# Second attention of a hybrid encoder step: values as the stationary operand for pairs of heads, normalised by a block diagonal product

## The reference, cut to what matters

```python
def stick_breaking(q, k, v, qpos, kpos):              # 8 heads of 64
    z = einsum('bqhd,bkhd->bhqk', q, k) * B_DIM ** -0.5
    before = kpos[None, :] < qpos[:, None]
    log_keep = where(before, log_sigmoid(-z), 0.0)
    rev = cumsum(log_keep, axis=3, reverse=True)
    after = concatenate([rev[..., 1:], zeros_like(rev[..., :1])], axis=-1)
    a = where(before, exp(log_sigmoid(z) + after), 0.0)
    return einsum('bhqk,bkhd->bqhd', a, v)

oa = rms(oa) * p['g_sub_a'] * (1.0 - lam_init)        # first attention, 4 heads of 128
ob = rms(ob) * p['g_sub_b']                           # rms over the 64 elements of one head
o = concatenate([oa.reshape(b, t, 512), ob.reshape(b, t, 512)], axis=-1) @ p['w_out']
x = x + g1 * o
```

## Time and profile before

| | |
|---|---|
| median of 3 runs | 1126.28 us (1124.11 to 1126.4) |
| profiled execution | 1125.94 us, span 1124.1 us |
| PE busy | 1060.9 us (94%) |
| PEld busy | 661.9 us (59%) |
| DVE busy | 395.1 us (35%) |
| ACT busy | 276.9 us (25%) |
| POOL busy | 293.7 us (26%) |
| mean granted clock of TensorE | 0.988 of full speed |
| second attention, from its first scores | 252.24 to 348.66 us of the span |

### The profile page before, as it was taken

The page is one execution under the profiler, slowest core; times in us unless marked ns, Lnnn a source line. Parts: engine busy times, 40 slices in busy tenths (PEclk is TensorE's granted clock), DMA queues, the critical chain, the costliest instruction groups (busy, mean ns, idle before and its releaser), DMA issues.

```text
span 1124.1 us, 19352 instructions
## 1 busy us (share of the span) xinstructions
PE 1060.9 (94%) x6520; PEld 661.9 (59%) x6521; DVE 395.1 (35%) x954; ACT 276.9 (25%) x735; POOL 293.7 (26%) x494
## 2 busy tenths in 40 slices
PE   3999999999998999999999999989999999999994
PEld 1677755556765447765656555656666565656541
DVE  3633301655754227422222222222222222222447
ACT  3200004667653005012111111111111111111232
POOL 1000002003521000523434334334433434333300
PEclk9999999999999999999999999999999999999997
DMA  8722245007740008479899999999999999998394
GB/s 333 286 75 75 76 169 183 1 1 286 281 150 1 1 0 314 193 313 392 321 336 416 415 415 415 414 415 401 380 356 359 407 413 414 415 400 349 121 418 119
DMA packets 77649, 304.26 MB, mean 271 GB/s; under 512 B 13302, under 2 KB 15416, under 8 KB 59496
## 3 DMA queue, kind: packets, MB, share of 16 engines
q1 hardware_dynamic: 60696, 268.26, 61.2%
q0 software_dynamic: 16256, 33.08, 7.8%
q10 hardware_dynamic: 656, 2.36, 0.5%
HBM read 290.26 MB, written 33.82 MB: 288 GB/s over the span
## 4 chain that ended last, share of the span: by engine, by line
PE 56%; DMA 4%; SPq 4%; issue 2%; DVE 1%; POOL 1%; ACT 1%; ACTq 0%; POOLq 0%; DVEq 0%
PE bank L1100 24%; PE bank L1107 13%; PE bank L1022 5%; DMA arena<-in_w_down 4%; PE bank L1093 3%; PE bank L1174 3%; PE bank L1112 2%; PE bank L1165 1%; SPq L384 1%; SPq L383 1%; PE bank L708 1%; PE bank L709 1%; POOL arena L561 1%; SPq L387 1%; PE bank L954 1%
## 5 line engine op out<-in xcount | busy, mean ns | idle before, releaser
L1100 PE MATMUL bank<-arena 128*64 128x256 f32 x2880 | 332.3, 382 | 16.4 <-issue 8.7
L1100 PEld LDWEIGHTS bank<-arena 128*64 128x64 f32 x2880 | 248.2, 138 | 123.6 <-issue 67.3
L1918 DVE COPY arena<-bank 128x512 f32<-128x512 f32 x90 | 62.2, 691 | 328.7 <-PE bank L1093 328.7
L1107 PE MATMUL bank<-arena 128*64 128x512 f32 x728 | 176.3, 601 | 1.5 <-DVE arena L1912 0.6
L1429 ACT COPY arena<-bank 128x128 f32<-128x128 f32 x90 | 23.9, 266 | 413.4 <-PE bank L1112 413.4
L576 POOL DMA_INDIRECT arena<-h_rows,arena x93 | 98.4, 1058 | 82.7 <-POOL arena L573 78.2
L584 POOL DMA_INDIRECT y_rows<-arena x91 | 93.4, 1026 | 85.7 <-POOL arena L581 79.3
L757 PE MATMUL bank<-arena 128*128 128x288 f32 x448 | 108.9, 406 | 0.3 <-DVE arena L1578 0.3
L757 PEld LDWEIGHTS bank<-arena 128*128 128x128 f32 x448 | 85.0, 190 | 24.5 <-issue 1.1
L1912 DVE COPY arena<-bank 128x512 f32<-128x512 f32 x91 | 62.9, 691 | 102.2 <-PE bank L1107 102.2
L1107 PEld LDWEIGHTS bank<-arena 128*64 128x64 f32 x728 | 52.1, 136 | 67.1 <-issue 66.4
(11 more groups left out here) (289 smaller groups left out, 1100.4 us busy)
## 6 DMA issues: line engine op xcount, KB each, us to landing
arena<-in_w_gate SPq DMA_DIRECT2D x64, 1024.0 KB, 12.7
arena<-in_w_up SPq DMA_DIRECT2D x64, 1024.0 KB, 15.4
arena<-in_w_down SPq DMA_DIRECT2D x64, 1024.0 KB, 14.5
arena<-in_w_ada SPq DMA_DIRECT2D x8, 2048.0 KB, 12.0
arena<-in_w_in SPq DMA_DIRECT2D x5, 2048.0 KB, 8.1
arena<-y_rows SPq DMA_DIRECT2D x3, 3072.0 KB, 16.7
arena<-in_w_ada SPq DMA_DIRECT2D x8, 1024.0 KB, 17.8
arena<-in_w_out SPq DMA_DIRECT2D x2, 2048.0 KB, 9.7
```

Of the source, the lines that this page charges most:

```text
L1100: last = pe.matmul(bank[0][n * SLOT:n * SLOT + SLOT, 0:2 * P].rearrange("p (g f) -> p g f", f=P), HGT[:, k % 4, k // 4, :], w[:, :, n * P: ...
L1107: last = pe.matmul(bank[3][n * SLOT:n * SLOT + SLOT, :], AE[:, f, :], DN[j][:, f, 512 * n:512 * n + 512], start=(f == 0), stop=(f == 1))
L1918: dve.tensor_copy(hgt, bank[1][:, :]).then_inc(hgt_ready, 1)
```

## The change

The weights A of a head are in SBUF with keys on the partitions. Before, A was the stationary operand and the head's values V (64 columns) the moving one, ten products for each head. Now `pair_values(p)` makes V stationary (128x64) and streams A (512, 384, 256 and 128 columns for the four key blocks), with the two heads of a pair in the two column halves of the array, so the outputs come out transposed in bank 7: head elements on the partitions, 512 queries on the free dimension.

ScalarE copies them straight to OT (`pair_out`, 128x512). VectorE squares them into SQ, TensorE multiplies SQ by PAIR, a block diagonal matrix of 1/64 (`pair_squares`), which puts each head's mean square on all its partitions, ScalarE takes Ln and then Exp with scale -0.5 (`pair_root`), and VectorE multiplies output, root and gain (`pair_norm`). The transposes of k = 4 to 7 of the prompt and their copies go, as do all `b_mean`, `b_rms`, `b_norm` of the prompt heads; the sample keeps the old way.

TensorE's order for a pair is now `b_scores`, `pair_values(p-1)`, `ada` twice, `b_sums` twice, `pair_squares(p-1)`. ScalarE does `pair_root(p-1)` after the pair's last Exp, VectorE `pair_norm(p-2)` and `pair_square(p-1)` after the pair's logarithms. Pair 3's values come after `b_scores(8)`, its squares after `b_sums(8)` and ahead of the gate rows, its root on ScalarE ahead of the sample's copies.

```diff
@@ TensorE
+            def pair_values(p):
+
+                if p:
+                    pe.wait_ge(pair_ln, PAIR_BASE + p)
                 else:
                     pe.wait_ge(proj_dve, NT)
-                if h in (HB - 2, HB - 1):
+                if p == HB // 2 - 1:
                     unread(7)
+                pe.wait_ge(at_ready, 6 * p + 6)
+                for j in range(4):
+                    for h in (2 * p, 2 * p + 1):
+                        o = h % 2 * DB
+                        last = pe.matmul(bank[7][o:o + DB, j * P:TP], V[:, j, 512 + h * DB:512 + h * DB + DB], AT[:, h % 2, ZO[j]:ZO[j] + ZW[j]],
+                                         start=(j == 0), stop=(j == 3), skip_group_check=True)
+                last.then_inc(pvb_done, 1)
+
+            def pair_squares(p):
+
+                pe.wait_ge(ob_evac, p + 1)
+                pe.wait_ge(pair_sq, PAIR_BASE + p + 1)
+                pe.matmul(bank[7][:, :], PAIR, SQ, start=True, stop=True).then_inc(pair_ms, 1)
...
                 if p:
-                    b_values(2 * p - 1)
+                    pair_values(p - 1)
...
-                if p < HB // 2 - 1:
-                    b_values(2 * p)
+                if p:
+                    pair_squares(p - 1)
             b_scores(HB)
-            b_values(HB - 2)
+            pair_values(HB // 2 - 1)
             ada_turn_later()
-            b_values(HB - 1)
             b_sums(HB)
+            pair_squares(HB // 2 - 1)
...
-            turn(OA, 1, half=(on_ready, NT + HB), sample=(on_ready, NT + HB + 1))
+            for k in range(4):
+                turn_chunk(OA, k, 2)
+            turn_sample(OA, (on_ready, NT + 1))
             turned(1)
+            pe.wait_ge(pair_ready, PAIR_BASE + HB // 2)
@@ ScalarE
+            def pair_out(p):
+                act.wait_ge(pvb_done, p + 1)
+                act.copy(OT[:, 4 + p, 0:TP], bank[7][:, :]).then_inc(ob_evac, 1)
+
+            def pair_root(p):
+
+                act.wait_ge(pair_ms, PAIR_BASE + p + 1)
+                act.activation(SQ, bank[7][:, :], ACT.Ln, bias=EPST[:, 0:1]).then_inc(pair_ln, 1)
+                act.wait_ge(pair_ln, PAIR_BASE + p + 1)
+                act.activation(SQ, SQ, ACT.Exp, scale=-0.5).then_inc(pair_rs, 1)
...
                 if p:
-                    b_out(2 * p - 1)
+                    pair_out(p - 1)
                 b_exp(2 * p)
                 b_exp(2 * p + 1)
-                if p < HB // 2 - 1:
-                    b_out(2 * p)
+                if p:
+                    pair_root(p - 1)
             b_fade(HB)
-            b_out(HB - 2)
+            pair_out(HB // 2 - 1)
             b_log(HB)
-            b_out(HB - 1)
             b_exp(HB)
-            b_out(HB)
+            pair_root(HB // 2 - 1)
+            b_out()
@@ VectorE
+            dve.memset(EPST, EPS)
+            for o in (0, DB):
+                dve.memset(PAIR[o:o + DB, o:o + DB], 1.0 / DB)
+                dve.memset(PAIR[o:o + DB, DB - o:P - o], 0.0)
...
+            def pair_square(p):
+
+                dve.wait_ge(ob_evac, p + 1)
+                o = OT[:, 4 + p, 0:TP]
+                dve.tensor_tensor(SQ, o, o, ALU.mult).then_inc(pair_sq, 1)
+
+            def pair_norm(p):
+
+                dve.wait_ge(pair_rs, PAIR_BASE + p + 1)
+                o = OT[:, 4 + p, 0:TP]
+                dve.scalar_tensor_tensor(out=o, in0=o, scalar=GA[:, 1:2], in1=SQ, op0=ALU.mult, op1=ALU.mult).then_inc(pair_ready, 1)
+                dve.wait_ge(pair_ready, PAIR_BASE + p + 1)
...
+                if p >= 2:
+                    pair_norm(p - 2)
                 if p:
-                    b_mean(2 * p - 2)
-                    b_mean(2 * p - 1)
-                if p >= 2:
-                    b_norm(2 * p - 4)
-                    b_norm(2 * p - 3)
+                    pair_square(p - 1)
...
             b_keep(HB)
-            b_mean(HB - 2)
-            b_mean(HB - 1)
-            b_norm(HB - 2)
-            b_norm(HB - 1)
+            pair_square(HB // 2 - 1)
+            pair_norm(HB // 2 - 1)
             b_mean(HB)
```

More of the change, by code:

```diff
@@ L158, in build @@
         GA = at(take(2), 2)
+        PAIR = at(take(P), P)
+        EPST = at(take(1), 1)
         SS = at(take(NT), NT)
@@ L265, in build @@
         z_half = sem("z_half")
+        pair_sq, pair_ms, pair_ln, pair_rs, pair_ready = ada_ld[0], ada_ld[1], ada_ld[6], ada_ld[7], in0_ld[0]
+        PAIR_BASE = 16
         abs_ready, fade_ready, ls_ready, z_done, lk_ready, p_done, eb_done, at_ready, pvb_done, ob_evac, lk_ln = map(
@@ L624, in back, with turn_chunk, turn @@
                 return last
-            def turn_chunk(src, k):
+            def turn_chunk(src, k, step=1):
                 for t in range(4):
                     last = pe.transpose(bank[k % 4][:, t * P:t * P + P], src[:, t, k * P:k * P + P], IDENT)
-                last.then_inc(tr_done, 1)
-            def turn(src, r, half=None, sample=None, begun=0, only_prompt=False):
+                last.then_inc(tr_done, step)
+            def turn(src, r, begun=0, only_prompt=False):
                 for k in range(begun, KC):
-                    if k == 4 and half:
-                        pe.wait_ge(*half)
                     if k >= 4:
@@ L642, in turn @@
                 if not only_prompt:
-                    turn_sample(src, sample)
+                    turn_sample(src)
             def turn_sample(src, sample=None, odd_apart=False):
@@ L955, in on_rows, with b_values @@
                 return last
-            def b_values(h):
-                if h >= 1:
-                    pe.wait_ge(ob_evac, h)
+            def pair_values(p):
+                if p:
+                    pe.wait_ge(pair_ln, PAIR_BASE + p)
                 else:
                     pe.wait_ge(proj_dve, NT)
-                if h in (HB - 2, HB - 1):
+                if p == HB // 2 - 1:
                     unread(7)
[L965 to L972, removed]
+                pe.wait_ge(at_ready, 6 * p + 6)
[9 more added lines that the diff above has]
+                pe.matmul(bank[7][:, :], PAIR, SQ, start=True, stop=True).then_inc(pair_ms, 1)
+            def b_values(h):
+                pe.wait_ge(pair_ln, PAIR_BASE + HB // 2)
+                pe.wait_ge(at_ready, 3 * HB + 1)
+                if h == HB:
                     pe.wait_ge(eb_done, 3 * HB + 3)
@@ L1205, in squares, with turned @@
                 act.activation(junk[0:r, :], X[0:r, t, :], ACT.Square, accum_out=SS[0:r, t:t + 1]).then_inc(done, 1)
-            def turned(r, dst, scale, shift, ks=range(1, KC, 2)):
+            def turned(r, dst, scale, shift, ks=range(1, KC, 2), step=1):
                 for k in ks:
-                    act.wait_ge(tr_done, 9 * r + k + 1)
+                    act.wait_ge(tr_done, 9 * r + step * (k + 1))
                     if scale:
@@ L1214, in turned @@
                         ins = act.copy(dst[:, k, 0:TP], bank[k % 4][:, :])
-                    ins.then_inc(tr_act, 1)
+                    ins.then_inc(tr_act, step)
             act.wait_ge(smt_ready, 1)
@@ L1340, in b_exp, with b_out @@
                     if h >= 2 and x == 0:
-                        act.wait_ge(pvb_done, h - 1)
+                        act.wait_ge(pvb_done, h // 2)
                     act.activation(AT[0:r, h % 2, o:o + w], b[0:r, 0:w], ACT.Exp).then_inc(eb_done, 1)
[L1344 to L1350, removed]
+            def pair_out(p):
[6 more added lines that the diff above has]
+                act.activation(SQ, SQ, ACT.Exp, scale=-0.5).then_inc(pair_rs, 1)
+            def b_out():
+                act.wait_ge(pvb_done, HB // 2 + 1)
+                act.copy(OA[0:TS, 4, 512:768], bank[7][0:TS, 0:256])
+                act.copy(OA[0:TS, 4, 768:D], bank[7][TS:P, 0:256]).then_inc(ob_evac, 1)
             for p in range(HB // 2):
@@ L1507, in norm, with turned @@
                 dve.tensor_scalar(XN[0:r, t, :], X[0:r, t, :], RS[0:r, t:t + 1], None, ALU.mult).then_inc(xn_ready, 1)
-            def turned(r, dst, scale, shift, ks=range(0, KC, 2)):
+            def turned(r, dst, scale, shift, ks=range(0, KC, 2), step=1):
                 for k in ks:
-                    dve.wait_ge(tr_done, 9 * r + k + 1)
+                    dve.wait_ge(tr_done, 9 * r + step * (k + 1))
                     if shift:
@@ L1515, in turned @@
                     elif scale:
-                        dve.tensor_scalar(dst[:, k, 0:TP], bank[k % 4][:, :], scale(k, 0), None, ALU.mult).then_inc(tr_dve, 1)
+                        dve.tensor_scalar(dst[:, k, 0:TP], bank[k % 4][:, :], scale(k, 0), None, ALU.mult).then_inc(tr_dve, step)
                     else:
                         dve.tensor_copy(dst[:, k, 0:TP], bank[k % 4][:, :]).then_inc(tr_dve, 1)
-                if r == 2 or KC - 2 not in ks:
+                if r == 2 or ks[-1] != (2 if r == 1 else KC - 2):
                     return
@@ L1738, in b_norm @@
             def b_norm(h):
-                dve.wait_ge(orb_ready, h + 1)
```

(1 more changed line is left out.)

18 lines of the change are left out of this document (6 added, 12 removed).

## The result

| | before | after |
|---|---|---|
| median | 1126.30 us (8 runs) | 1133.74 us (8 runs, 1131.67 to 1140.49) |
| ratio, 95% interval | | 1.0079 (1.0063 to 1.0095) |
| profiled execution / its span | 1125.94 / 1124.1 | 1132.37 / 1130.6 |
| PE busy | 1060.9 | 1057.9 |
| ACT busy | 276.9 | 289.4 |

The change makes the kernel slower by 7.4 us, going by the medians. (The ratio gives 8.9 us, since two of the eight times are 1137.50 and 1140.49.) In the windows by stage the reader is to see first that the pairs are as forecast, and then the clock. They answer to the earlier trace rows: pairs 1, 2 and 3, the sample's scores up to `b_sums(8)`, from there to the end of the sample's values, and the turn with the second gate rows. Columns are length, busy PE, PEld, DVE, ACT, POOL, granted clock, DMA share, GB/s.

A forecast was written before the change was run, and what follows sets the result against it. TensorE was taken as busy throughout the attention, with the logarithm chain ending within 0.1 us of it. Pairs -0.20, sample +1.03, turn -0.33 gave +0.5; one clock fall, 1.6, made +2.1: 1128.4 us, range 1124.5 to 1132.

The forecast's parts named there:

- tiles not side by side: Rival: the two halves of `pair_values` run one after the other, 4.4 us instead of 2.36; 1133.4 us, chance 0.04.
- TensorE's work, the pairs: Attention pairs: TensorE's own work falls some 8.8 us, but waits for VectorE and ScalarE leave the four pairs at -0.20.
- TensorE keeps its savings: Rival: the logarithms don't bind, so TensorE's 8.8 us are kept, 1117.5, or half, 1122; chance 0.12.
- Table loads: ScalarE's root in each pair: two table loads, one before Ln and one before Exp, 1.28 us each.
- Sample part and turn without the clock: Sample part +1.03 us, with 3.35 idle ahead of `b_sums(8)`; turn -0.33 us, from 16 fewer transposes.
- A fall costs 1.6: One added fall to 1.2 GHz behind the sample part's idle stretch: 16 products take 3.63 us instead of 2.05.
- Bounds 0 to 3.2: Clock term: 0 if the fall is missed, 3.2 if it also catches pair 1's stall or lasts longer in the turn.
- a bound and a rival: Longer or further falls, in pair 1 or the turn: bound 3.2 us; rival up to 1.6 more, 1130.0, chance 0.16.
- no further fall: Rival: the sample part's idle stretch is split so that the clock stays; +0.5, 1126.8 us, chance 0.20.
- one load: Rival: ln then exp need one table load, so each root is 1.28 us or more shorter; 1127.1, chance 0.03.
- savings case: Rival that TensorE's savings are kept in full (1117.5 us) or half (1122); chance 0.12, of which 0.09 counted as faster.
- half of the forecast: Whole kernel: half the forecast's 0.45 chance, counted as within 0.2% (2.25 us), since its centre is 2.1.

The follow-up runs named there:

- e7_root_joined: Changed kernel rescheduled: square ahead of `a_norm`, root's Ln and Exp in the next pair's phases, pair 3's squares and first gate rows ahead of `b_sums(8)`; 1124.79 us.
- e1_fill_sums: Changed kernel plus three unread filler products of 512 columns in the idle stretch ahead of `b_sums(8)`; 1130.26 us, ratio 1.0046 to the kernel before.
- e5_fill_square: `e2_fill_both` with `pair_square(0)` moved ahead of `a_norm` on VectorE in pair 1; 1126.83 us, ratio 1.0011 to the kernel before.
- e9_after_again: The changed kernel, unaltered, run once more for a second profile beside the kernel before on one chip; 1135.39 us, ratio 1.0085.
- e8_early_output: `e7_root_joined` with the first rows' output projection (k = 4 to 7) begun in the turn, and chunk copies reassigned; 1117.70 us, ratio 0.9938 to the kernel before.
- e6_gate_rows_first: Changed kernel with the first gate rows moved from behind `pair_squares(3)` to ahead of `b_sums(8)`; 1130.69 us, ratio 1.0047 to the kernel before.
- e10_full_first: Changed kernel plus two whole-array filler products of 512 columns between the idle stretch and `b_sums(8)`; 1137.11 us, ratio 1.0091 to the kernel before.
- e2_fill_both: `e1_fill_sums` plus filler products in the turn, ahead of and behind the sample's transposes; 1128.53 us, ratio 1.0023 to the kernel before.

## Why the prediction was wrong

The range ended at 1132.0 and the median is 1133.74; the forecast of +2.1 was of the right sign, and small by 5.3. One rival had the number almost exactly, "tiles not side by side" with 1133.4, and is wrong all the same: it wanted 4.4 us for `pair_values`, which took 2.31.

- **TensorE's work, the pairs.** Right. `pair_values` takes 2.30 to 2.31 us to the next line's start (2.36 forecast); pairs 1 to 3 took 18.42, 16.46 and 17.41 against 18.18, 16.48 and 17.47; the four pairs together -0.05 against -0.20. The waits are those named: 1.80 for line 1758 (the square behind `a_norm`), 1.18 for line 1728 in pair 3. The rival that TensorE keeps its savings falls for this order of work. It is not the logarithms that forbid it: with the root out of the way `e7_root_joined` keeps 3.3 us in the pairs.
- **Table loads.** Right: each root has two, at 1.28 us. The rule of the Trainium skill ("ScalarE: Activation LUTs", "Table sets: the hidden batching unit") gives one for ln and exp together; these rows of the profile after, counting the loads of the root's Ln and of its Exp, disagree:

```profile
L1363 ACT ACT_TABLE_LOAD  x4: 1283/1283/1283, 285.6 to 348.0; - x4
...
L1365 ACT ACT_TABLE_LOAD  x4: 1283/1283/1283, 288.6 to 350.0; - x4
```

- **Sample part and turn without the clock.** Right, by the windows. TensorE idles 3.06 us ahead of `b_sums(8)` (3.35 forecast); with cover (`e1_fill_sums`) it is 27.8 us from the scores to the end of the values (27.66 forecast). From there to the second gate rows it is 7.57 us, 0.35 shorter than the 7.92 before (0.33 forecast). With the pairs that is -0.05 + 1.13 - 0.35 = +0.7 where the sum had +0.5. The 0.75 us of `e5_fill_square` look like the same number and are luck: that run also lacks the stall of pair 1 and the fall in the turn, and in its profile the projection's last part starts at 412.96, 2.2 us ahead of the kernel before.
- **The step that failed: the price of a fall.** "A fall costs 1.6" came from one stretch of 3.4 us, that of the kernel before. The place and the trigger were right, the size was not: over `b_sums(8)` it cost 3.3 us in one profile and 6.5 in another. "Bounds 0 to 3.2" therefore bounded the count of falls, and their length in the turn only. The fall in the turn grew as well, from 3.4 to 6.8 us, and took 1.05 us of the projection, which I had only as a bound and a rival. Adding 3.3 to 6.5, and 1.0, to the 0.5 gives 4.8 to 8.0. That holds the 7.4 measured; it does not hold the 10.2 of `e9_after_again`, where the projection's last part starts 8.1 us later than before and the rest is not placed. Why the same fall lasts 3.4 us in one place and 13.7 in another stays open.
- **Where the savings went.** From the first scores to the projection PE's busy time fell from 104.4 to 100.1 us. Counted at the full clock it is some 7.9 us less (an estimate, with half of the low busy time taken off both), near the 8.8 forecast; over the whole kernel it fell by 3.0 only, since low-clock products last longer. The savings were turned into waits, and `e7_root_joined` and `e8_early_output`, which keep the new form and lose most of the waits, show that these belong to the order of the work.
- **The chances.** Those of faster, within 0.2% and slower do not follow from their parts. Within 0.2% lie no further fall 0.20, one load 0.03, the rest of the savings case 0.03 and half of the forecast 0.22, so 0.48 and not 0.43; slower is then 0.43, not 0.48.

## What to carry to other kernels

When work is taken off an engine that is always busy, find what the removed instructions had covered: here 3.2 us of filler and values had hidden the sample's logarithms, and taking them away bought an idle stretch and a slow clock behind it. Do not price a clock fall by the one low stretch in the trace: here it cost 1.6 us in one place and 3.3 to 6.5 in another. Put useful work, or even a product that nobody reads, into TensorE's gaps. In these traces waits of 1.6 us and more were followed by falls, some of them each time and some in one execution of several; waits of 1.18 us were not. No length was shown to be safe, as the falls over the first scores came behind waits of 0.60 us. A new operation on an engine with two phases of functions belongs in those phases: the root cost 2.6 us of table loads for each pair where it first stood, and none one phase later.

## What was not expected of the hardware

The same program in two executions had low stretches of 6.8 and 13.7 us behind the same idle stretch of 3.06 us, with TensorE busy all through them. The changed kernel's times spread over 8.8 us (1131.67 to 1140.49), where the kernel before spreads over 3.3. The low stretches may be the reason; that is not shown, as only one of the eight executions has a profile. After 1.80 us idle in pair 1 the clock stayed up in the two profiles of the changed kernel and in those of `e1_fill_sums`, `e6_gate_rows_first` and `e10_full_first`, and went down in that of `e2_fill_both`.

The column halves of `pair_values` do hide their weight loads. The profile after has 64 loads and 64 products on line 968, 16 of each for a pair, in 2.31 us from the first product to the next line:

```profile
L968 PEld LDWEIGHTS bank<-arena x64: 132/137/137, 271.8 to 333.5; 128*64 128x64 f32 x64
```

16 loads of 0.137 us would be 2.2 us by themselves, and the products, 5120 columns in all at the 7.02/32 = 0.22 us for 512 of line 1040 (also in column halves), another 2.2. The Trainium skill ("TensorE: Matmul & The Clock Gate", "Part 3: Packing small matmuls — row/col tiling") says that a load overlaps a running product only where the row groups differ; here they are the same 128 rows, and the trace disagrees. The same section also names loads into the background weight buffer as pulled ahead of running products, which the trace would fit.
